# First parts of x and first weight unit moved into the end of the softmax ahead

## The reference, cut to what matters

```
z = x @ w_in                     # 1024 x 6564, cut into the inputs of four branches and the gate logits
y_a = mla(...)                   # softmax attention over the low-rank inputs
y_b = stick_breaking(...)
y_c = conformer_conv(...)
y_d = forgetting_attention(...)  # softmax attention with a forget gate
gates = sigmoid(gate_logits + b_gate)
proj = einsum('bsnc,ncd->bsnd', ys, w_branch)     # four products of 256 x 1024
merged = sum(proj * gates, axis=2)
mix = merged @ w_o
```

## Time and profile before

| | us |
|---|---|
| timed runs, median of 3 | 2955.39 (2952.82 to 2955.53) |
| profiled execution, whole | 2951.99 |
| its span, first to last instruction | 2950.3 |
| mean granted clock of PE | 0.948 of full |
| PE busy | 2593.1 |
| DVE busy | 1584.6 |
| ACT busy | 1294.9 |

### The profile page before, as it was taken

The page is one execution under the profiler, slowest core; times in us unless marked ns, Lnnn a source line. Parts: engine busy times, 40 slices in busy tenths (PEclk is TensorE's granted clock), DMA queues, the critical chain, the costliest instruction groups (busy, mean ns, idle before and its releaser), DMA issues. The chain is left out here.

```text
span 2950.3 us, 31869 instructions
## 1 busy us (share of the span) xinstructions
PE 2593.1 (88%) x11300; PEld 1827.9 (62%) x11300; DVE 1584.6 (54%) x2343; ACT 1294.9 (44%) x1976; POOL 255.3 (9%) x197
## 2 busy tenths in 40 slices
PE   6899887899999898899986899878978999698997
PEld 2577664577777575477764555545746777455554
DVE  6545575322233456434456777644664345577775
ACT  6333544422223435433324777624353323277773
POOL 0000000000000010000002333201000000033230
PEclk9899998999999999899997999989999999799998
DMA  9412000322123111122135999751302122299994
GB/s 345 143 58 86 5 1 1 107 93 85 43 86 118 58 58 58 44 71 81 62 131 167 327 307 318 259 192 43 109 6 86 65 79 88 91 307 320 322 324 173
DMA packets 263283, 392.20 MB, mean 133 GB/s; under 512 B 23663, under 2 KB 185471, under 8 KB 263167
## 3 DMA queue, kind: packets, MB, share of 16 engines
q1 hardware_dynamic: 236448, 340.55, 34.5%
q10 hardware_dynamic: 14367, 33.34, 3.0%
q0 software_dynamic: 12352, 16.81, 1.8%
HBM read 386.44 MB, written 29.36 MB: 141 GB/s over the span
## 5 line engine op out<-in xcount | busy, mean ns | idle before, releaser
L193 PE MATMUL banks<-ring_parts,arena_parts 128*80 128x512 f32 (+2 forms) x1296 | 515.8, 398 | 0.0
L192 PE MATMUL banks<-arena_parts,hT_parts 128*128 128x512 f32 x1056 | 423.8, 401 | 41.1 <-DVE ring_parts L222 21.7
L194 PE MATMUL banks<-arena_parts,ring_parts 128*128 128x512 f32 (+1 forms) x1168 | 457.9, 392 | 0.0
L222 DVE TENSOR_TENSOR ring_parts<-ring,hT_parts 128x1024 fp32r<-128x1024 f32 x148 | 181.4, 1226 | 393.6 <-ACT hT_parts L218 390.9
L2991 DVE TENSOR_TENSOR ring_parts<-ring,hT_parts 128x2048 fp32r<-128x2048 f32 x128 | 292.7, 2288 | 155.5 <-ACT hT_parts L2885 155.2
L192 PE MATMUL banks<-hT_parts,arena_parts 128*80 128x512 f32 (+1 forms) x824 | 336.7, 409 | 37.7 <-DVE hT_parts L2988 21.7
L218 ACT ACTIVATE hT_parts<-ring 128x1024 fp32r<-128x1024 f32 x148 | 156.6, 1058 | 453.9 <-PE banks L194 453.1
L193 PE MATMUL banks<-hT_parts 128*128 128x512 f32 x864 | 344.5, 399 | 0.0
L2885 ACT ACTIVATE hT_parts<-ring 128x2048 fp32r<-128x2048 f32 x128 | 244.4, 1911 | 207.0 <-DMA ring<-in_w_exp_up 155.7
L192 PE MATMUL banks<-arena_parts 128*128 128x512 f32 (+3 forms) x712 | 280.5, 394 | 8.7 <-DVEq L161 3.8
L192 PEld LDWEIGHTS banks<-arena_parts,hT_parts 128*128 128x128 f32 x1056 | 200.9, 190 | 101.5 <-issue 43.5
(11 more groups left out here) (486 smaller groups left out, 3930.7 us busy)
## 6 DMA issues: line engine op xcount, KB each, us to landing
ring<-in_w_exp_gate SPq DMA_DIRECT2D x64, 1024.0 KB, 5.8
ring<-in_w_exp_up SPq DMA_DIRECT2D x64, 1024.0 KB, 8.9
ring<-in_w_exp_down SPq DMA_DIRECT2D x128, 512.0 KB, 7.3
ring<-in_w_in SPq DMA_DIRECT2D x58, 1024.0 KB, 7.3
ring<-in_w_mod SPq DMA_DIRECT2D x24, 1024.0 KB, 13.7
ring<-in_w_gate SPq DMA_DIRECT2D x11, 1024.0 KB, 5.5
ring<-in_w_up SPq DMA_DIRECT2D x11, 1024.0 KB, 8.3
ring<-in_w_down SPq DMA_DIRECT2D x22, 512.0 KB, 4.4
```

Of the source, the lines that this page charges most:

```text
L192: nc.tensor.matmul(out, lh, rh, start=start and i == 0, stop=False)
L193: nc.tensor.matmul(out, lh, rl, start=False, stop=False)
L194: last = nc.tensor.matmul(out, ll, rh, start=False, stop=stop and i == len(terms) - 1)
L222: nc.vector.tensor_tensor(unit_of(ring_r, n, q), unit_of(ring, n, q), hi_unit(s[1]).bitcast(F32), ALU.subtract).then_inc(S("unit_lo"), 1)
```

## The change

The split of x parts 0 and 1 and of unit 0 moves from the start of the projections and of the gates to the end of the softmax ahead. On ACT it stands behind the last softmax piece (and behind `forget_act`) and ahead of the two copies into `yT`; on DVE behind the last softmax piece and ahead of `forget_dve`. To make room, `px_hi` and `px_lo` change places in memory, and the 2 that PE adds to `unit_used` moves to the start of the layer. In the gates, parts 2 and 3 and unit 1 now come first, then the four loads of branch weights, then parts 4 to 7.

```
-        px_hi = [A_r(1024 + LAT * k, LAT) for k in range(6)] + [A_r(19516 + LAT * k, LAT) for k in range(2)]
-        px_lo = [A_r(20540 + LAT * k, LAT) for k in range(KD)]
+        px_hi = [A_r(1024 + LAT * k, LAT) for k in range(4)] + [A_r(19516 + LAT * k, LAT) for k in range(4)]
+        px_lo = [A_r(3072 + LAT * k, LAT) for k in range(2)] + [A_r(20540 + LAT * k, LAT) for k in range(2, KD)]
...
+            pe.sem_inc(S("unit_used"), 2)          # mla_pe, at its start; gone from pj_pe
             landed(pe, N_Z0, R)
...
             if nm == "mla":
                 forget_act(act)
+            joint(act)
             for r in range(2):
                 act.wait_ge(S(nm + "_pv"), 2 * r + 2)
                 nc.scalar.activation(yT[:, branch, r, :], ps[:, 4 + r, :], ACT.Copy)
...
+            joint(dve)
             if nm == "mla":
                 forget_dve(dve)
...
+        def pj_first_act(act, R):
+            parts_hi(act, "px", px_hi[0:2], hT_lat[0:2])
+            split_hi(act, N_CV, 0, R, (0, 0))
+
+        def pj_first_dve(dve):
+            parts_lo(dve, "px", px_hi[0:2], hT_lat[0:2], px_lo[0:2])
+            split_lo(dve, N_CV, 0, (0, 0))
+
+        def gate_first_act(act, R):
+            parts_hi(act, "gx", gx_hi[0:2], hT_lat[0:2])
+            split_hi(act, N_GT, 0, R, (U_GT, 0))
+
+        def gate_first_dve(dve):
+            parts_lo(dve, "gx", gx_hi[0:2], hT_lat[0:2], hT_lo[0:2])
+            split_lo(dve, N_GT, 0, (U_GT, 0))
...
         def gate_act(act, lay, R):
+            def split(c, q):
+                split_hi(act, N_GT + c, q, R, (U_GT + 4 * c + q, q))
+
+            parts_hi(act, "gx", gx_hi[2:4], hT_lat[2:4])
+            split(0, 1)
             act.wait_ge(S("out_done"), 16 * LT * lay + 1)
             for br in range(4):
                 act.dma_start(w_br[:, br, :, :], ...).then_inc(S("wbr_in"), 16)
-
-            def split(c, q):
-                split_hi(act, N_GT + c, q, R, (U_GT + 4 * c + q, q))
-
-            parts_hi(act, "gx", gx_hi[0:2], hT_lat[0:2])
-            split(0, 0)
-            parts_hi(act, "gx", gx_hi[2:], hT_lat[2:])
+            parts_hi(act, "gx", gx_hi[4:], hT_lat[4:])
...
-            parts_lo(dve, "gx", gx_hi[0:2], hT_lat[0:2], hT_lo[0:2])
-            split(0, 0)
-            parts_lo(dve, "gx", gx_hi[2:], hT_lat[2:], hT_lo[2:], 2)
+            parts_lo(dve, "gx", gx_hi[2:4], hT_lat[2:4], hT_lo[2:4], 2)
+            split(0, 1)
+            parts_lo(dve, "gx", gx_hi[4:], hT_lat[4:], hT_lo[4:], 4)
```

More of the change, by code:

```diff
@@ L1910, in soft_pe, with soft_act @@
             values(H2 - 1)
-        def soft_act(act, nm, p, pt, scale, branch):
+        def soft_act(act, nm, p, pt, scale, branch, joint):
             def turned(u):
@@ L1936, in soft_act, with soft_dve @@
                 nc.scalar.activation(yT[:, branch, r, :], ps[:, 4 + r, :], ACT.Copy)
-        def soft_dve(dve, nm, p, scale):
+        def soft_dve(dve, nm, p, scale, joint):
             V = nc.vector
@@ L1952, in soft_dve @@
                     V.tensor_scalar(p[:, c, 0:w], p[:, c, 0:w], stat[:, 6 + c:7 + c], None, ALU.mult).then_inc(S(nm + "_pn"), 1)
+            joint(dve)
             if nm == "mla":
                 forget_dve(dve)
+        def pj_first_act(act, R):
[10 more added lines that the diff above has]
+            split_lo(dve, N_GT, 0, (U_GT, 0))
         pj_jobs = ((N_CV, (2, 3, 0, 1)), (N_SB, (0, 1, 2, 3)), (N_VV, None), (N_FX, (0, 1, 2, 3)))
         def pj_pe(pe, R):
-            pe.sem_inc(S("unit_used"), 2)
             for c, (n, tiles) in enumerate(pj_jobs):
@@ L1998, in pj_act @@
             split = pj_split_act(act, R)
-            parts_hi(act, "px", px_hi[0:2], hT_lat[0:2])
-            split(0, 0)
             parts_hi(act, "px", px_hi[2:], hT_lat[2:])
@@ L2051, in split_and_tap @@
                 conv_taps(dve, tap_at(c, q), tap_at(c, q) + 2)
-            parts_lo(dve, "px", px_hi[0:2], hT_lat[0:2], px_lo[0:2])
-            split(0, 0)
             parts_lo(dve, "px", px_hi[2:], hT_lat[2:], px_lo[2:], 2)
@@ L2311, in gate_run @@
         def gate_run(c, split, merged_part, branch_parts):
-            split(c, 1)
+            if c:
+                split(c, 1)
             if c == 7:
@@ L3239, in _ @@
                     rendezvous(act, "act")
-                    soft_act(act, "mla", mla_p, mla_pt, MD ** -0.5, 0)
+                    soft_act(act, "mla", mla_p, mla_pt, MD ** -0.5, 0, lambda e: pj_first_act(e, R))
                     rendezvous(act, "act")
@@ L3245, in _ @@
                     rendezvous(act, "act")
-                    soft_act(act, "fox", fox_p, fox_pt, 1.0, 3)
+                    soft_act(act, "fox", fox_p, fox_pt, 1.0, 3, lambda e: gate_first_act(e, R))
                     rendezvous(act, "act")
@@ L3283, in _ @@
                     rendezvous(dve, "dve")
-                    soft_dve(dve, "mla", mla_p, MD ** -0.5)
+                    soft_dve(dve, "mla", mla_p, MD ** -0.5, pj_first_dve)
                     rendezvous(dve, "dve")
@@ L3289, in _ @@
                     rendezvous(dve, "dve")
-                    soft_dve(dve, "fox", fox_p, 1.0)
+                    soft_dve(dve, "fox", fox_p, 1.0, gate_first_dve)
                     rendezvous(dve, "dve")
```

## The result

| | before | changed |
|---|---|---|
| timed runs, median | 2955.39 us (5 runs, 2943.12 to 2956.73) | 2923.37 us (5 runs, 2920.10 to 2929.70) |
| profiled execution's span | 2950.3 | 2920.3 |
| mean granted clock of PE | 0.948 | 0.957 |

The ratio is 0.9903, with a 95% interval of 0.9884 to 0.9921: 28.7 us faster (23 to 34); the two medians differ by 32.0 us. I had forecast 17.4 us, with 2932 us as the lower end of the range.

What follows compares the result with a forecast made beforehand. PE, busy 88% of the span, was taken to bound the kernel. Gates 11.4, clock 4.85 and projections 1.2 made 17.4 us, from 2955.39 to 2938.0 us; forecast 2937.5, range 2932 to 2946 (8 in 10).

Steps and rivals of the forecast that it cites:

- The chain moves ahead of ACT's copies, and PE starts 5.7 us earlier at the gates: Forgetting softmax to gates: splitting two parts and one unit starts at ACT's first copy; 11.4 us in two layers.
- The clock stays up over a gap of 1.0 us, 4.85 us: First gate matmuls: PE stands still 1.0 us, not 6.6, and keeps full clock; 4.85 us in both layers together.
- The rival of a fallen clock: At the gates the clock still falls; gain only 12.5 us, time 2943 us; chance 0.15.
- the first of the two rules: PE's clock anywhere: it drops after an idle stretch; by this the 4.85 us at the gates come in full.
- the second rule: PE's clock anywhere: many small pauses can make it swing as well; by this the 4.85 us don't come.
- The branch weights: no stall: Gate stage: the four later loads still give parts by 1261.4 to 1263.3, PE wanting them at 1262.7; no stall taken.
- the early end of the issue times: Gate stage: ACT's sequencer runs ahead of its data path, so branch loads start some 0.2 us behind the rendezvous.
- The projections: 0.6 us each, DVE's forget gate being late: MLA softmax to projections: DVE does chain, then forget gate, 3.36 + 1.91 us serially; PE's wait 3.6 us, not 4.2.
- Does it last: "so the stage moves as a block": Gate and expert stages: PE and the weight stream it releases move along, so the gain lasts to the end.
- an argument on pauses: Layer 0's forgetting softmax, first half at 0.51 with PE busy: a short gap alone doesn't prove a full clock.
- a changed clock elsewhere: Other stages: the clock falls otherwise, or expert loads come no earlier; fewer than 6 of 17 us left, 2951; chance 0.04.
- 4 us for one clock: First projection matmuls: the clock also stays up there, 4 us more, time 2933.5 us; chance 0.08.

Runs made afterwards that it cites:

- b4: The changed kernel with the four loads of branch weights behind unit 2 instead of unit 1: 2937.70 us, ratio 0.9953 to the kernel before.
- c1: The changed kernel with the forget gate moved from the MLA softmax's end into the projections: 2915.44 us, ratio 0.9887 to the kernel before.
- a3: The change at the gates alone, the hand-over to the projections as in the kernel before: 2935.03 us, ratio 0.9948 to the kernel before.
- a4: The change at the projections alone, the gates as in the kernel before: 2942.18 us, ratio 0.9975 to the kernel before.
- b1: The changed kernel with one more ACT copy at the end of the stick-breaking stage: 2929.32 us, ratio 0.9933 to the kernel before.
- c3: The changed kernel with the branch-weight loads first in the gate stage, ahead of parts 2 and 3 and unit 1: 2923.59 us, ratio 0.9913 to the kernel before.
- b2: The kernel before with two more matmuls at the end of the stick-breaking stage: 2946.35 us, ratio 0.9992 to the kernel before.
- c2: c1 with two more matmuls at the end of the stick-breaking stage: 2918.31 us, ratio 0.9895 to the kernel before.
- a2: The kernel before measured again, nothing changed: 2950.47 us, ratio 1.0003.

## Why the prediction was wrong

- *The chain moves ahead of ACT's copies, and PE starts 5.7 us earlier at the gates.* Right: the wait went from 6.6 to 0.9 us, and DVE arrives last, as written.
- *The clock stays up over a gap of 1.0 us, 4.85 us.* Right: 1.00 in both layers. The rival of a fallen clock is out. The trace agrees here with the first of the two rules cited from the Trainium skill ("TensorE: Matmul & The Clock Gate", Part 1: The HAM clock gate). That rule alone doesn't cover layer 0's forgetting softmax in the kernel before: its clock fell at 1201.3, and the longest pause of PE in the 11 us ahead was 1.0 us. Whether the second rule is at work there no run shows.
- *The branch weights: no stall.* Right, with the early end of the issue times; the landing took 14.0 us from the first issue and not 13.1, ACT waited 1.45 us, and the parts were done at 1250.7 where PE wanted them at 1251.5. b4 shows the price beyond that point: 3.6 us of stall in layer 0 and some 3 us more by the clock.
- *The projections: 0.6 us each, DVE's forget gate being late.* Right: 3.44 us of wait in place of 4.24, the clock still low at the start. c1 shows that the forget gate held it.
- *Does it last: "so the stage moves as a block".* This step failed. The hand-overs gave 17.1 us, against 17.4 in the sum, and everything else was taken to keep its length. It doesn't: with the new hand-over to the projections layer 0's forgetting softmax, which starts 0.5 us earlier, lost its 20 us at half clock and 8.4 us of its length (a3 and a4 tell the two hand-overs apart). That the earlier start is what does it is likely and not shown: the one run that was to move the start alone, b1, also moved PE's pause, and in layer 1 the start's distance from the layer's beginning doesn't sort the long cases from the short ones. The gain was luck as far as the forecast goes: b4 and c3, which change only the gate stage, found the same stretch at half clock in layer 1. I had that row in hand (1201 to 1222 at 0.51), and used it as an argument on pauses, but gave a changed clock elsewhere only as a loss, with a chance of 0.04, and not as a gain. The other 4.5 us of the difference between the spans are a low clock in layer 1's stick-breaking and in the first block, less and more in the experts; the same stages varied as much between profiles of one kernel (turn stage 17.6 and 19.4 us, layer 1's stick-breaking 61.9 and 64.3 us in two profiles of the changed one), so these I put down to scatter.
- *The range.* Its lower end held 4 us for one clock and 2.7 us for the spread of three runs. The runs of one kernel spread over 20 us in later measurements.

By the profiles the 8.4 us of the softmax and the 17.1 us of the hand-overs are 25.5 us, inside the measured 23 to 34. That the 8.4 us stand in the time, and not only in the profile, rests on a4, which gained 7 us where its own hand-over was worth 1.2; b2 removed the same stretch and gained 2 us, 7 at most, so their full size in the time isn't shown. The halves measured alone, 15 and 7 us, add up to 23, the whole to 29; the intervals (10 to 21 and 4 to 11) allow the difference, and I didn't settle whether there is more to it.

## What to carry to other kernels

Before adding up what a move saves, list the stretches behind it that run at half clock without an idle PE: each may vanish, or a new one appear, when something ahead of it shifts by a few tenths of a microsecond. Here one such stretch was worth 8.4 us, against 15.9 and 1.2 us of the two hand-overs. Where two engines have work to do while a third makes the last products of a stage, the first operands of the next stage belong there; and what is only needed later (here the forget gate) must go out of that place. Try such an edit with a dummy of a few tenths of a microsecond ahead of the sensitive stage, to see what is the edit and what the clock, and read PE's pause there too, since the dummy changes it as well.

## What was not expected of the hardware

- An ACT copy of 0.38 us ahead of a softmax of 37.5 us made it 46.0 us, in both layers (b1). In the kernel before, two matmuls of 0.23 us removed the same slow stretch, with the stage starting at the same place (b2); in c2 they didn't keep it away.
- In layer 0, from the MLA inputs to the forgetting softmax, the stage lengths of unchanged code repeat to 0.1 us between profiles, the low clock included, although the stages ahead of them differ by up to 1 us: the three profiles with the old hand-over to the projections and nothing added (before, a2, a3) had the low clock at the same distance from the first block's end (239.2, 239.3 and 239.1 us). In layer 1 they repeat less well: stick-breaking took 61.9 and 64.3 us in two profiles of the changed kernel.
- In that softmax PE counts as busy all the time at half clock (20.40 of 20.40 us); many of its matmuls are small (4 rows for the forget terms). A busy share near 1 doesn't show that the clock is up.
